# More products of constants around the gathered sums of an expert stage, and the first slot's products ahead of the second slot's turn

## The chip, the core and the metric

The kernel runs on one core of one Trainium2 chip. The metric is the device time of one execution in microseconds, the median of several runs. TensorE, VectorE (DVE in the profile), ScalarE (ACT), GpSimd (POOL) and the SP queue each work through a list of their own; they wait for each other by semaphores only. The granted clock of TensorE in the profile is a share of 2.4 GHz: 1.00 is 2.4 GHz, 0.50 is 1.2 GHz.

## What is computed

Two blocks of two transformer layers each, float32, batch 1, 256 tokens, model width 1024. The first block has two kinds of attention and a dense MLP per layer. The second has a pooling layer and an attention layer, each followed by a mixture of experts, and it is in these two mixtures that the change lies:

```python
def hier_moe(h, w_rg, b_rg, w_re, b_re, w_gate, w_up, w_down):
    ...
    gates = jnp.sum(jax.nn.one_hot(expert_id, N_EXPERTS, dtype=jnp.float32) * e_w[..., None], axis=1)
    a = jnp.einsum('nd,edf->nef', hf, w_gate)
    b = jnp.einsum('nd,edf->nef', hf, w_up)
    hid = jax.nn.silu(a) * b * gates.astype(h.dtype)[..., None]
    return jnp.einsum('nef,efd->nd', hid, w_down).reshape(shp)
```

Each token has two experts out of 16 (both in one of four groups), each expert 256 hidden columns. In layer 0 the mixture has 512 tokens (the latent set and the context set, four tiles of 128), in layer 1 it has 256 (two tiles).

## The kernel before

Every engine has a program of its own, and the order of its work is written out by hand; a claim of a PSUM bank waits for whoever read the bank last (`claim`, `freed`).

An expert stage (`moe`, L1045 for TensorE, L1621 for ScalarE, L2300 for VectorE, L2522 for GpSimd) works in slots of 128 rows: 23 slots in layer 0, 19 in layer 1. Slots 0 to 15 are one expert each; further slots take what is over and gather their weights too. First the tokens are routed and their rows written to memory. Then for each slot s:

- GpSimd gathers 128 token rows into `h_row[s % 3]` (L2534), three slots ahead; the gather for slot s + 3 waits until the turning of slot s has read its buffer.
- TensorE turns them, 8 transposes into PSUM banks 0 and 1 (`turn_rows`, L1089, instructions at L1094). It claims both banks, so it waits for VectorE's reading of the slot before.
- ScalarE copies the turned rows to the high part (`rows_high`, L1646) and VectorE subtracts to get the low part (`rows_low`, L2306).
- TensorE multiplies with the gate and up weights (`gates_and_ups`, L1098): for each of 8 pieces of the depth a product high by high, low by high and high by low, 24 in all. The low parts of the rows are waited for before the third product.
- ScalarE's tanh, two steps of VectorE and a turning of the hidden values follow, and the down products (`downs`) of slot s stand behind the gate and up products of slot s + 1.

Weights come through a ring of four buffers `raw`, filled by the SP queue; ScalarE rounds them (`round_expert`) and VectorE splits off the low part (`split_expert`, L1874). For the first slots ScalarE's and VectorE's order is written out ahead of the loop.

After the last slot GpSimd gathers, for each tile of 128 tokens, the two expert rows of each token (`both`, L2569). ScalarE scales the first by its gate, VectorE adds the second (L2353), TensorE turns the sum (8 transposes at L1166), and VectorE adds it into x (`add_tile`, 8 instructions at L2347). In layer 0 ScalarE then squares x and TensorE sums the squares over features (`sum_tile`, 8 one-column matmuls for each tile, 16 instructions in the profile), and `norm` spreads the reciprocal root. In layer 1 TensorE turns x back and ScalarE copies it out (`store`).

`idle(b, n)` (L665) issues n products of constants, 128 by 512, into bank b, which nobody reads. Each shows as two instructions. One such block of 8 stands after the last slot. All matmuls are issued from the helper at L663.

Of the kernel before, what the change touches and what calls it, by code (L numbers as in the profile page):

```python
# [322 lines left out]
def build(nc, a, out):  # L323
    with ExitStack() as ctx:
# [330 lines left out]
        def tensor_program(e):  # L655
            freed = {}

            def claim(b):
                for sig, name in freed.pop(b, ()):
                    e.wait_ge(*sig.at(*name))  # L660
# [4 lines left out]
            def idle(b, n):  # L665

                claim(b)
                for _ in range(n):
                    mm(psum[:, b, :], ident, cst[:, C_ROT1:C_ROT1 + 512], True, True)
# [329 lines left out]
            s = split_slot(g)  # L999
# [45 lines left out]
            def moe(layer):  # L1045
# [43 lines left out]
                def turn_rows(s):  # L1089
                    claim(0)  # L1090
                    claim(1)
                    e.wait_ge(*in_h_row[s % 3].at(layer, s))
                    for k in range(DT):
                        d = e.transpose(psum[:, k // 4, k % 4 * P:(k % 4 + 1) * P], h_row[:, s % 3, k:D:DT], ident)  # L1094
                    d.then_inc(*turned.on("row", layer, s))
                    freed[0] = freed[1] = [(rest, ("ht", layer, s))]
# [47 lines left out]
                    freed[5] = freed[6] = [(copied, ("y", layer, s))]  # L1144

                turn_rows(0)
                turn_rows(1)
                for s in range(slots + 1):
                    if s < slots:
                        gates_and_ups(s)  # L1150
                    if s:
                        turn_hidden(s - 1)
                    if s + 2 < slots:
                        turn_rows(s + 2)
                    if s:
                        downs(s - 1)

                idle(7, 8)

                for i in range(T):  # L1160
                    b = 2 * (i % 2)
                    claim(b)
                    claim(b + 1)
                    e.wait_ge(*shaped.at("both", layer, i))
                    for k in range(DT):
                        d = e.transpose(psum[:, b + k // 4, k % 4 * P:(k % 4 + 1) * P],  # L1166
                                        both[:, 2 * i, k * P:(k + 1) * P], ident)
                    d.then_inc(*turned.on("both", layer, i))
                    freed[b] = freed[b + 1] = [(added, ("both", layer, i))]
                    if layer == 0 and i:  # L1170
                        sum_tile(i - 1)
                    if layer == 1 and i:
                        store(i - 1)
                if layer == 0:
                    sum_tile(T - 1)
                    norm(("q", 0))
                    idle(4, 1)
                else:
                    store(T - 1)
# [154 lines left out]
        def scalar_program(e):  # L1334
# [286 lines left out]
            def moe(layer):  # L1621
                stage = ("e", layer)
                T, slots = 2 * len(NORMS[stage][0]), SLOTS[layer]
                for t in range(DT):
                    modulate(stage, t)
                e.wait_ge(*turned.at("logit_rows", layer))
                e.activation(logit_rows[0:20, 0:T * P], psum[0:20, 4, 0:T * P], ACT.Copy).then_inc(
                    *copied.on("logit_rows", layer))
                for i in range(T):
                    b = 2 * (i % 2)  # L1630
                    o = tmp[:, 2 * i:2 * i + 2, :]
                    e.wait_ge(*turned.at("h_row", layer, i))
                    e.activation(o, psum[:, b:b + 2, :], ACT.Copy).then_inc(*copied.on("h_row", layer, i))
                    e.wait_ge(*copied.at("h_row", layer, i))
                    e.dma_start(h_dram[layer][i * P:(i + 1) * P, :], o.rearrange("p b c -> p (b c)")).then_inc(
                        *h_kept.on(layer, i))
                e.wait_ge(*routed.at("shifted", layer))
                e.activation(ROUTE[layer]["eg"], ROUTE[layer]["d4"], ACT.Exp).then_inc(*expd.on("group", layer))
                e.wait_ge(*routed.at("dm", layer))
                e.activation(ROUTE[layer]["ex"], ROUTE[layer]["dm"], ACT.Exp).then_inc(*expd.on("pair", layer))  # L1640
                if layer == 1:
                    e.wait_ge(*multiplied.at(WO + 3))
                round_expert("g", layer, 1)
                round_expert("u", layer, 1)

                def rows_high(s):  # L1646
                    e.wait_ge(*turned.at("row", layer, s))
                    e.activation(ht_hi[:, s % 2], psum[:, 0:2, :].rearrange("p b (k c) -> p (b k) c", c=P),
                                 ACT.Copy).then_inc(*rounded.on("ht", layer, s))

                e.wait_ge(*routed.at("all", layer))
                rows_high(0)
                rows_high(1)
                for s in range(slots + 1):
                    if s < slots:
                        e.wait_ge(*multiplied.at("gu", layer, s))
                        e.activation(tmp[:, s % 2, 0:UC], psum[:, 2 + s % 2, 0:UC], ACT.Tanh, scale=0.5).then_inc(
                            *copied.on("tanh", layer, s))
                    if s:
                        at_ = (s - 1) % 2  # L1660
                        e.wait_ge(*turned.at("hid", layer, s - 1))
                        e.activation(ut_all[:, at_, :], psum[:, 4, 0:P], ACT.Copy).then_inc(  # L1662
                            *copied.on("ut", layer, s - 1))
                        e.activation(ut_hi[:, at_, :], psum[:, 4, P:2 * P], ACT.Copy).then_inc(
                            *rounded.on("ut", layer, s - 1))
                    if s + 2 < slots:
                        rows_high(s + 2)
                        round_expert("g", layer, s + 2)
                    if s < slots:
                        round_expert("d", layer, s)  # L1670
                    if s + 2 < slots:
                        round_expert("u", layer, s + 2)
                    if s:
                        at_ = (s - 1) % 2
                        e.wait_ge(*multiplied.at("d", layer, s - 1))
                        if s >= 3:
                            e.wait_ge(*y_kept[at_].at(layer, s - 3))
                        e.activation(y_row[at_][:], psum[:, 5:7, :].rearrange("p b c -> p (b c)"), ACT.Copy).then_inc(
                            *copied.on("y", layer, s - 1))
                        e.wait_ge(*copied.at("y", layer, s - 1))  # L1680
                        e.dma_start(y_dram[layer][(s - 1) * P:s * P, :], y_row[at_][:]).then_inc(
                            *y_kept[at_].on(layer, s - 1))
                if layer == 0:
                    feed(QKV - 1)

                def square_tile(i):
                    e.wait_ge(*added.at("both", 0, i))
                    e.activation(tmp[:, 2 * i:2 * i + 2, :].rearrange("p b (k c) -> p (b k) c", c=P),
                                 x[:, :, i * P:(i + 1) * P], ACT.Square).then_inc(*copied.on("sq_tile", i))

                def store(i):
                    e.wait_ge(*turned.at("out", i))
                    e.activation(tmp[:, 2 * i:2 * i + 2, :], psum[:, 4 + 2 * i:6 + 2 * i, :], ACT.Copy).then_inc(
                        *copied.on("out", i))

                for i in range(T):
                    e.wait_ge(*in_both[i].at(layer, 1))
                    e.activation(both[:, 2 * i, :], both[:, 2 * i, :], ACT.Copy,
                                 scale=gate_w[:, 0, i:i + 1]).then_inc(*copied.on("both", layer, i))
                    if layer == 0 and i:  # L1700
                        square_tile(i - 1)
                if layer == 0:
                    square_tile(T - 1)
                    norm_root(("q", 0))
                else:
                    for i in range(T):
                        store(i)
# [97 lines left out]
        def vector_program(e):  # L1805
# [494 lines left out]
            def moe(layer):  # L2300
# [9 lines left out]

                rows_low(0)
                split_expert("g", layer, 1)
                rows_low(1)
                split_expert("u", layer, 1)
                for s in range(slots + 1):
                    if s:
                        at_ = (s - 1) % 2
# [335 lines left out]
```

## Time and profile before

| | us |
|---|---|
| median of 3 runs | 1694.5 (1692.42 to 1698.91) |
| the profiled execution, device time | 1690.77 |
| its span in the profile | 1689.0 |
| granted clock, mean | 0.951 |
| TensorE busy | 1523.5 (90%) |
| VectorE busy | 1284.8 (76%) |
| ScalarE busy | 859.9 (51%) |
| GpSimd busy | 222.9 (13%) |

Times in the text are microseconds from the start of the span. A row of the timeline gives start, duration, engine, line, operation, output and inputs with their shape, how many instructions were merged into it, and in brackets how long the engine had been idle and what ended that. Durations of merged rows run from the first start to the last end.

### The profile page before, as it was taken

To read this page: it belongs to the slowest core of one execution; us is meant where nothing else is said; L and a number is where in the kernel's file an instruction comes from. 1 tells how busy PE (TensorE), PEld (TensorE's weight loads), DVE (VectorE), ACT (ScalarE), POOL (GpSimd) and SP (SyncE) were. 2 spreads that over 40 slices of the span, in tenths; PEclk is the share of its full clock that TensorE was granted. 3 is DMA by queue.
4 is the path that set the end of the run, shared out by engine and by line. 5 is a ranking of instruction groups with operands and counts; after the bars stand their busy time and mean duration, and the time that the engine had idled before them with its cause. 6 is when DMAs were issued, how large, how long until landed. Compare 5 with 4: busy or idle time off the path is not lost.

```text
span 1689.0 us, 24256 instructions
## 1 busy us (share of the span) xinstructions
PE 1523.5 (90%) x9830; PEld 1295.2 (77%) x9830; DVE 1284.8 (76%) x1882; ACT 859.9 (51%) x1186; POOL 222.9 (13%) x201
## 2 busy tenths in 40 slices
PE   3999989999999987999998889989979889799996
PEld 2889878999888977899887567767668547577764
DVE  4968878787877988899885668877658883588872
ACT  2546435444444642544444447766534464377762
POOL 5040010000004000000000311013220300311021
PEclk9999999999999998999999889999969899899998
DMA  9753687899763555578772369999965531599973
GB/s 324 267 170 128 222 299 265 299 325 313 269 200 126 176 174 194 191 268 279 263 259 75 125 224 415 422 413 358 363 219 200 179 121 50 209 393 423 423 307 137
DMA packets 191871, 424.99 MB, mean 252 GB/s; under 512 B 8344, under 2 KB 136784, under 8 KB 175504
## 3 DMA queue, kind: packets, MB, share of 16 engines
q1 hardware_dynamic: 170688, 334.53, 55.6%
q0 software_dynamic: 13824, 63.61, 10.1%
q10 hardware_dynamic: 7248, 25.30, 3.7%
q8 instruction: 78, 1.28, 0.3%
q14 instruction: 33, 0.27, 0.0%
HBM read 397.19 MB, written 26.21 MB: 251 GB/s over the span
## 4 chain that ended last, share of the span: by engine, by line
PE 57%; DVE 24%; DMA 7%; ACT 7%; issue 3%; POOL 1%; SPq 0%; POOLq 0%; ACTq 0%; DVEq 0%
PE psum L663 54%; DVE acc L1871 6%; DVE w_lo L1850 6%; DMA h_row<-h_rows,token_at 3%; PE psum L1094 2%; DVE gu_lo L1883 2%; ACT w_hi L1361 2%; DMA raw<-in_w_ada 1%; ACT att_room L1783 1%; DVE tmp L2054 1%; DVE tmp L1904 1%; ACT gu_hi L1375 1%; DVE stats L2060 1%; DMA dn_raw<-in_moe_wd 1%; DVE h_lo L1913 1%
## 5 line engine op out<-in xcount | busy, mean ns | idle before, releaser
L1850 DVE TENSOR_TENSOR w_lo<-raw,w_hi 128x1024 fp32r<-128x1024 f32 x250 | 302.2, 1251 | 66.3 <-ACT w_hi L1361 66.2
L663 PE MATMUL psum<-h_lo,w_hi 128*128 128x256 f32 (+1 forms) x1280 | 339.5, 289 | 2.8 <-DVE h_lo L2099 2.8
L663 PE MATMUL psum<-h_hi,w_lo 128*128 128x256 f32 (+1 forms) x1280 | 339.3, 288 | 0.2 <-DVE w_lo L1850 0.2
L1871 DVE SCALAR_TENSOR_TENSOR acc<-raw,cond,acc 128x1024 f32<-128x1024 f32 x224 | 294.5, 1324 | 11.5 <-DMA raw<-in_w_ada 6.5
L1361 ACT ACTIVATE w_hi<-raw 128x2048 fp32r<-128x2048 f32 x125 | 238.8, 1912 | 121.3 <-PE psum L663 90.1
L663 PE MATMUL psum<-h_hi,w_hi 128*128 128x256 f32 (+1 forms) x1280 | 262.9, 298 | 18.0 <-DVE tmp L2082 14.5
L663 PEld LDWEIGHTS psum<-h_lo,w_hi 128*128 128x128 f32 x1280 | 248.8, 194 | 4.3 <-DVE h_lo L2099 3.0
L663 PEld LDWEIGHTS psum<-h_hi,w_lo 128*128 128x128 f32 x1280 | 248.9, 194 | 2.0 <-DVE w_lo L1850 0.6
L663 PEld LDWEIGHTS psum<-h_hi,w_hi 128*128 128x128 f32 x1280 | 199.2, 196 | 39.1 <-issue 16.3
L1883 DVE TENSOR_TENSOR gu_lo<-raw,gu_hi 128x1024 fp32r<-128x1024 f32 x160 | 188.7, 1221 | 27.7 <-ACT gu_hi L1375 27.7
L1375 ACT ACTIVATE gu_hi<-raw 128x2048 fp32r<-128x2048 f32 x84 | 159.7, 1905 | 0.8 <-PE psum L663 0.8
L663 PE MATMUL psum<-gu_lo,ht_hi 128*128 128x512 f32 x336 | 132.4, 394 | 0.0
L663 PE MATMUL psum<-gu_hi,ht_lo 128*128 128x512 f32 x336 | 132.2, 393 | 0.0
L663 PE MATMUL psum<-u_lo,w_hi 128*128 128x256 f32 x448 | 121.7, 288 | 9.3 <-DVE u_lo L2127 9.3
L663 PE MATMUL psum<-gu_hi,ht_hi 128*128 128x512 f32 x336 | 126.2, 396 | 0.0
L663 PE MATMUL psum<-u_hi,w_lo 128*128 128x256 f32 x448 | 121.1, 287 | 0.0
L2438 POOL TENSOR_TENSOR tmp<-tmp 128x256 f32<-128x256 f32 (+1 forms) x28 | 29.9, 1069 | 543.0 <-ACT tmp L1386 542.9
L663 PE MATMUL psum<-u_hi,w_hi 128*128 128x256 f32 x448 | 100.4, 290 | 0.0
L663 PEld LDWEIGHTS psum<-u_lo,w_hi 128*128 128x128 f32 x448 | 87.8, 196 | 10.3 <-DVE u_lo L2127 10.3
L663 PE MATMUL psum<-dn_raw,ut_all 128*128 128x512 f32 x168 | 83.1, 618 | 5.6 <-ACT ut_all L1662 5.3
L663 PEld LDWEIGHTS psum<-u_hi,w_lo 128*128 128x128 f32 x448 | 87.7, 196 | 0.0
L1386 ACT ACTIVATE tmp<-x 128x256 f32<-128x256 f32 (+1 forms) x56 | 25.8, 476 | 104.0 <-DVE x L1984 90.7
(259 smaller groups left out, 2771.2 us busy)
## 6 DMA issues: line engine op xcount, KB each, us to landing
raw<-in_w_ada SPq DMA_DIRECT2D x48, 1024.0 KB, 6.6
raw<-in_w_mod SPq DMA_DIRECT2D x48, 1024.0 KB, 5.6
raw<-in_w_in SPq DMA_DIRECT2D x34, 1024.0 KB, 5.7
raw<-in_w_up SPq DMA_DIRECT2D x32, 1024.0 KB, 5.5
raw<-in_w_down SPq DMA_DIRECT2D x32, 1024.0 KB, 6.8
raw<-in_moe_wg SPq DMA_DIRECT2D x32, 1024.0 KB, 11.5
raw<-in_moe_wu SPq DMA_DIRECT2D x32, 1024.0 KB, 10.4
dn_raw<-in_moe_wd SPq DMA_DIRECT2D x32, 1024.0 KB, 10.1
```

What stands on the lines that cost most here:

```text
L663: return e.matmul(o, lhs, rhs, start=start, stop=stop, skip_group_check=True)
L1094: d = e.transpose(psum[:, k // 4, k % 4 * P:(k % 4 + 1) * P], h_row[:, s % 3, k:D:DT], ident)
L1361: e.activation(flat_unit(w_hi[:, split_slot(u)]), raw[:, slot, :], ACT.Copy).then_inc(*w_rounded.on(u))
L1375: e.activation(gate_up(0, s, kind == "u"), raw[:, p % RAW_SLOTS, :].rearrange("p (k c) -> p k c", c=UC), ACT.Copy).then_inc(*w_rounded.on( ...
L1386: e.activation(tbuf(i, n), x[:, t, 0:n], ACT.Square).then_inc(*copied.on("sq", stage, t))
L1783: e.activation(att_room[:, h % 4, qt * S2:(qt + 1) * S2], psum[:, 2 * (h % 2) + qt, :], ACT.Exp, bias=st[:, 2 + qt:3 + qt], scale=scale[:, ...
L1850: e.tensor_tensor(flat_unit(w_lo[:, split_slot(u), k]), raw[:, slot, part], plain(flat_unit(w_hi[:, split_slot(u), k])), ALU.subtract).the ...
L1871: e.scalar_tensor_tensor(out=a_buf, in0=src[:, k, :], scalar=s, in1=a_buf, op0=ALU.mult, op1=ALU.add).then_inc(*mod_v.on(p, n, k))
L1883: e.tensor_tensor(gate_up(1, s, kind == "u")[:, k], src[:, k], plain(gate_up(0, s, kind == "u")[:, k]), ALU.subtract).then_inc(*w_rest.on( ...
L1904: e.scalar_tensor_tensor(out=tmp[:, t % 4, c], in0=x[:, t, c], scalar=gain_col(row, chunk + 1, t), in1=psum[:, 5, c], op0=ALU.mult, op1=AL ...
L1913: e.scalar_tensor_tensor(out=lo[:, t - 1, c], in0=tmp[:, (t - 1) % 4, c], scalar=column(row, chunk, t - 1), in1=plain(hi[:, t - 1, c]), op ...
L2438: e.tensor_tensor(o, o, tbuf(4 + (t + 1) % 4, n), ALU.add).then_inc(*pooled.on("sq", stage, t))
```

## The change

TensorE: slot 1's turning is issued behind slot 0's gate and up products. The block of constant products after the last slot grows from 8 to 15. One more constant product follows each turning of a gathered tile, in both layers; in layer 0 two more stand ahead of the last tile's sums and one ahead of the norm. ScalarE: the copy of slot 1's turned rows stands behind the tanh of slot 0. VectorE: the split of slot 1's up weights stands ahead of the subtraction for slot 1's rows. The results are the same.

```diff
@@ TensorE @@
                 turn_rows(0)
-                turn_rows(1)
                 for s in range(slots + 1):
                     if s < slots:
                         gates_and_ups(s)
+                    if s == 0:
+                        turn_rows(1)
                     if s:
                         turn_hidden(s - 1)
                     if s + 2 < slots:
...
-                idle(7, 8)
+                idle(7, 15)
...
                     d.then_inc(*turned.on("both", layer, i))
+                    idle(7, 1)
                     freed[b] = freed[b + 1] = [(added, ("both", layer, i))]
...
                 if layer == 0:
+                    idle(7, 2)
                     sum_tile(T - 1)
+                    idle(7, 1)
                     norm(("q", 0))
                     idle(4, 1)
@@ ScalarE @@
                 rows_high(0)
-                rows_high(1)
                 for s in range(slots + 1):
                     if s < slots:
                         e.wait_ge(*multiplied.at("gu", layer, s))
                         e.activation(tmp[:, s % 2, 0:UC], psum[:, 2 + s % 2, 0:UC], ACT.Tanh, scale=0.5).then_inc(
                             *copied.on("tanh", layer, s))
+                    if s == 0:
+                        rows_high(1)
@@ VectorE @@
                 rows_low(0)
                 split_expert("g", layer, 1)
+                split_expert("u", layer, 1)
                 rows_low(1)
-                split_expert("u", layer, 1)
```

## Rows read from the trace of the kernel before

**Rows 1.** The page, its chain that ended last: shares of the span by engine.
```profile
PE 57%; DVE 24%; DMA 7%; ACT 7%; issue 3%; POOL 1%; SPq 0%; POOLq 0%; ACTq 0%; DVEq 0%
```

**Rows 2.** The timeline (start, duration, what) at the start of layer 0's slots.
```profile
985.64 1.12 PE L1094 MATMUL psum<-cst,h_row 128*128 128x128 f32 x8
986.86 1.02 ACT L1648 ACTIVATE ht_hi<-psum 128x1024 fp32r<-128x1024 f32 x1 [12.52 <-PE psum L1094]
...
987.91 1.22 DVE L2308 TENSOR_TENSOR ht_lo<-psum,ht_hi 128x1024 fp32r<-128x1024 f32 x1 [5.41 <-ACT ht_hi L1648]
...
989.19 1.16 PE L1094 MATMUL psum<-cst,h_row 128*128 128x128 f32 x8 [2.43 <-DVE ht_lo L2308]
...
990.63 1.59 POOL L2535 DMA_INDIRECT h_row<-h_rows,token_at  x1 [2.18 <-PE psum L1094]
990.78 0.63 PE L663 MATMUL psum<-gu_hi,ht_lo 128*128 128x512 f32 x1
...
997.30 1.05 PE L1094 MATMUL psum<-cst,h_row 128*128 128x128 f32 x8
...
998.11 0.71 PE L663 MATMUL psum<-gu_hi,ht_hi 128*128 128x512 f32 x2
```

**Rows 3.** The timeline at the start of layer 1's slots.
```profile
1463.08 1.12 PE L1094 MATMUL psum<-cst,h_row 128*128 128x128 f32 x8 [1.59 <-DMA h_row<-h_rows,token_at]
...
1466.63 1.97 PE L1094 MATMUL psum<-cst,h_row 128*128 128x128 f32 x8 [2.43 <-DVE ht_lo L2308]
...
1469.26 0.63 PE L663 MATMUL psum<-gu_hi,ht_lo 128*128 128x512 f32 x1
```

**Rows 4.** Windows: stretch, length, busy PE, PEld, DVE, ACT, POOL (instructions), clock, DMA share, GB/s.
```profile
963.10:966.50 3.40, 3.40 (x26) 2.67 (x25) 2.88 (x16) 2.25 (x3) 0.00 (x0) 1.00 0.37 151
987.00:990.30 3.30, 1.11 (x9) 1.11 (x10) 2.39 (x3) 0.88 (x1) 0.94 (x1) 1.00 0.63 215
990.50:993.70 3.20, 3.20 (x9) 2.50 (x8) 3.15 (x3) 0.92 (x1) 1.59 (x1) 0.50 0.43 110
1465.00:1471.50 6.50, 4.87 (x16) 4.20 (x17) 5.29 (x5) 1.34 (x2) 1.87 (x2) 0.50 0.61 187
```

**Rows 5.** The timeline at the end of layer 0's experts.
```profile
1227.11 7.03 PE L663 MATMUL psum<-cst 128*128 128x512 f32 x16
...
1241.17 1.97 PE L1166 MATMUL psum<-cst,both 128*128 128x128 f32 x8 [7.03 <-DVE both L2353]
...
1243.93 2.15 DVE L2347 SCALAR_TENSOR_TENSOR x<-psum,mod,x 128x128 f32<-128x128 f32 x8
...
1252.75 3.57 PE L663 MATMUL psum<-cst,tmp 128*128 128x1 f32 x16
...
1254.97 2.15 DVE L2347 SCALAR_TENSOR_TENSOR x<-psum,mod,x 128x128 f32<-128x128 f32 x8
...
1258.17 2.16 DVE L2347 SCALAR_TENSOR_TENSOR x<-psum,mod,x 128x128 f32<-128x128 f32 x8 [1.05 <-PE psum L1166]
...
1265.82 2.08 PE L663 MATMUL psum<-cst,rstd_col 128*128 128x128 f32 x8 [0.56 <-DVE rstd_col L1890]
```

**Rows 6.** Windows, the same columns, the end of layer 0's experts.
```profile
1241.00:1266.00 25.00, 21.84 (x97) 20.18 (x98) 12.52 (x37) 9.00 (x9) 1.88 (x2) 0.50 0.70 251
```

**Rows 7.** The timeline at the end of layer 1's experts.
```profile
1663.45 7.03 PE L663 MATMUL psum<-cst 128*128 128x512 f32 x16
...
1676.41 1.97 PE L1166 MATMUL psum<-cst,both 128*128 128x128 f32 x8 [5.92 <-DVE both L2353]
...
1679.25 4.30 DVE L2347 SCALAR_TENSOR_TENSOR x<-psum,mod,x 128x128 f32<-128x128 f32 x16
```

**Rows 8.** Layer 0's later slots: TensorE's waits for gathered rows (sum, times, longest); gathers' landing.
```profile
PE psum L1094 <- DMA h_row<-h_rows,token_at: 6.2, 4, 4.8
DMA to landing us min/median/max: 6.9/8.4/12.6
```

**Rows 9.** Windows, the same columns, one slot in the middle of layer 1.
```profile
1532.20:1541.90 9.70, 9.70 (x45) 7.53 (x44) 8.12 (x10) 7.33 (x9) 0.94 (x1) 1.00 1.01 420
```

## The prediction

> **What bounds the kernel now.** I read the page first [rows 1]: TensorE carries 57% of the chain that ended last, so what counts is when TensorE's queue gets to go on. The change touches only the two expert stages, and each of them in two places: the start, where the rows of the first two slots are turned, and the end, where the experts' outputs are gathered and added. I read both places in the timeline and then the granted clock in the windows.
>
> At the start of layer 0 the turning of slot 0 runs at 985.64, and the turning of slot 1 only at 989.19, because both write PSUM banks 0 and 1: in between ScalarE copies (986.86, 1.02 us) and VectorE subtracts (987.91, 1.22 us), and TensorE waits 2.43 us [rows 2]. From one turning to the next it is 3.55 us. Layer 1 shows the same 3.55 us, 1463.08 to 1466.63 [rows 3]. Slot 0's own products stand behind slot 1's turning. The gap is followed by a stretch at a granted clock of 0.50, that is 1.2 GHz in place of 2.4: some 3.4 us in layer 0, and from 1465 to about 1471.7 in layer 1 [rows 4].
>
> At the end of layer 0 TensorE has nothing to do from 1234.14 (end of 8 products of constants, 7.03 us) until the first gathered and added tile is there at 1241.17 [rows 5]. From then to about 1270 it runs at 0.50 [rows 6]. But it isn't the bound of that loop: VectorE's first three additions into x start 5.52 us apart, the first at 1243.93, the third at 1254.97, in a ring VectorE, ScalarE's square, ScalarE's scaling, VectorE. Only the last addition (1258.17) waited for TensorE, 1.05 us, and behind it the sums and the norm are TensorE's own [rows 5]. Layer 1's end is short: the first turning starts at 1676.41, the two additions run from 1679.25 to 1683.55 [rows 7].
>
> **The start: slot 0's products ahead of slot 1's turning.** Gain: slot 0's products can start once ScalarE has copied row block 0. Two high products go, then the third, which reads the low part, waits for VectorE, whose subtraction ends at 989.13. So the third product starts where the second turning starts now, 989.2 in place of 990.78: 1.6 us earlier in layer 0 [rows 2]. In layer 1 it is 1466.6 in place of 1469.26, 2.6 us, but that time lies in the stretch at 0.50, which does half the work, so it is worth 1.3 us [rows 3, 4]. Loss: the turnings of slots 1 and 2 are now neighbours behind the products, and both write banks 0 and 1, so the 3.55 us from turning to turning stands there, where today no wait is (slot 2 is turned at 997.30 and the next products start at 998.11) [rows 2]. The wait has been moved, not removed, and the new one is whole, while the old one is only partly gone. Sum: 3.55 - 1.6 = +1.95 us in layer 0, 3.55 - 1.3 = +2.25 us in layer 1, together **+4.2 us**.
>
> Where the other queues are moved past: ScalarE's copy of slot 1 stands behind the tanh of slot 0 (0.38 us, started 0.2 us after the products end), which runs beside the turning (1.05 us): nothing. VectorE splits the second expert's up weights before slot 1's subtraction: these no longer wait 1.2 us, and their ring buffer is free for the SP queue that much earlier; no one waits for it. VectorE now sits waiting behind the split until slot 0's products are through, and queued behind that wait are the two steps of slot 0's hidden values (0.42 us each); they run while TensorE turns slot 2 and ScalarE copies it (2.1 us), and their reader comes a whole product block later: nothing. GpSimd's gather of row block 4 waits for slot 1's turning (now 990.63) and is issued some 8 us later, and its own queue with it; its reader is the turning of slot 4, behind two further blocks of products, at 9.70 us a slot some 16 us after the issue [rows 2, 9], and the longest landing of such a gather is 12.6 us [rows 8]: nothing. If the landing were longer the difference would be paid.
>
> The clock at the start. The trace has no wait between dense products of this length with both sides at 2.4 GHz, so I bound it. Today's stretches at 0.50 hold 3.2 us of TensorE's work in layer 0 and 4.9 us in layer 1, so they cost about 1.6 and 2.5 us [rows 4]. After the change the old gap is smaller (1.1 us, two products, 0.7 us) and may leave the clock up; the new gap of 2.43 us may drop it in slot 1's products. Both old dips gone and no new one: -4.1 us; both old ones kept and two new ones of 1.6 us: +3.2 us. A 2.43 us wait dropped the clock both times it is seen, so I expect the dips to move with the wait and take 0.
>
> Could the transfers hide the loss? In the loop TensorE is busy for all of the 9.70 us per slot and the DMA share is 1.01 beside it [rows 9]; later in layer 0 TensorE waits 6.2 us in all for gathered rows, and one gather took 12.6 us to land [rows 8]. A TensorE that comes 2 us later finds the queues that much less behind, if they never ran dry. But the share is only 0.43 to 0.63 around the start of both layers [rows 4], and the transfers are issued by the steps that come late. So between 0 and all of the 4.2 us hidden; I take 0.
>
> **The end: 7 more products before the first turning.** One costs 7.03 / 8 = 0.88 us, 0.86 from issue to issue. Seven take 6.0 us and end at 1240.1 in layer 0 (the wait ends at 1241.17) and, from 1663.45, at 1676.3 in layer 1 (1676.41): they fit, the second by 0.1 us [rows 5, 7]. If they end late, the first turning has room: it ends at 1678.4 and the addition starts at 1679.25, behind VectorE's own sum of the next tile. For the same reason a first turning in 1.1 in place of 1.97 us gains nothing in either layer. The cover of the seven is the gather; without it they would cost 6 us per layer.
>
> **The products between the tiles.** Layer 0 gets 1 after each turning, 2 before the last sum and 1 before the norm; layer 1 gets 1 after each turning. Clock held at 2.4 GHz through layer 0's end: a turning is 1.05 us, a product 0.86, a tile's sums half of 3.57, so TensorE needs 3.7 us of each 5.52. The sums of tile 2 start behind its square, about 1258.3, and end at 1260.1; two products, 1261.8; the last square is done by then (its addition starts at 1257.2); sums, 1263.6; a product, 1264.4; the norm starts there in place of 1265.82 and is 1.0 us shorter: **-2.5 us** [rows 5]. Clock left at 0.50: a turning 1.97, a product twice 0.86, the sums 3.57 [rows 5], together 7.2 us for a ring of 5.52, so TensorE becomes the bound: sums of tile 0 end at 1251.3, of tile 1 at 1258.5, of tile 2 at 1265.7, two products to 1269.1, sums to 1272.6, a product to 1274.3, norm there and not at 1265.82: **+8.5 us**. Which? Turnings and one-column sums alone have not raised it: 25 us at 0.50 with TensorE 87% busy [rows 6]. But four tiles turned with one product of constants in their middle stayed at 1.00 (963.1 to 966.5, the token rows being turned in the routing) [rows 4]. One product in every 5.5 us is between these two rows, so I expect the clock to fall at some tile and come back before the norm. I take +1 us, nearer to the held end.
>
> The Trainium skill, "TensorE: Matmul & The Clock Gate", Part 4 (PE-mode transpose), says that the full clock does not engage for transposes. The stretch from 1241 agrees (0.50 for 25 us); the row at 963.1 speaks against its strict form. By that rule the turnings would do nothing to hold the clock, and the end would come out at +8.5 in place of +1: rival B below.
>
> Layer 1's end: the output hangs on VectorE's second addition, which ends at 1683.55 [rows 7], and a store turning behind it. The product behind the second turning ends before the first addition does if the clock is held: 0. At 0.50 its 1.7 us delay both store turnings, the second of them too: up to +1.7 us. I take 0.
>
> **Sum**: +4.2 (start) + 0 (clock there) + 1 + 0 = +5.2 us on the profiled execution's own 1690.8 us, 1696.0 us. The median of the three runs lies 3.7 us above that execution; on it the forecast is 1694.5 + 5 = **1699.5 us**, slower by 0.3%, which a measurement of this kernel can barely tell (about 0.5%, 8.5 us, is its limit).
>
> **Rivals.** (A) The clock gains pay for the moved wait: held through layer 0's end (-2.5) and the old dips gone without new ones (-4.1), with +4.2: -2.4 us, 1692. For it: the gap is broken up and the 14 products of layer 0 fill waits. Against: the new wait is as long as the old. Chance 0.24. It ends on the other side of mine: faster than before, from the point where the end is held and more than 1.7 us of today's 4.1 us of dips is saved. (B) The products run at 0.50 and become the bound at the end of layer 0: 4.2 + 8.5 + up to 1.7, some +13 us, 1707.5; for it the 25 us at 0.50, against it the row at 963.1. Chance 0.17. (C) Transfers absorb the moved wait: +1 us, 1695.5, for it the share of 1.01 in the loop, against it the shares at the start. Chance 0.12. (D) The change does nothing that shows, as the seven products are hidden and the clock falls anyway: that is inside (C)'s time. My forecast (+2 to +8.5) has 0.47.
>
> **Range.** From A to near B: 1691 to 1707. Chances: faster by over 0.5% would need A and more, 0.04; slower by over 0.5% (above 1703) is B and the top of the forecast, 0.20; the rest 0.76.
>
> **What would show it.** In the profile after: in both layers turning 0, two products, a short stall, the rest of slot 0's products; then turning 1 and turning 2 with 3.55 us from start to start and a TensorE wait of about 2.4 us for VectorE's subtraction between them. Slot 1's products of layer 0 start 2 us later against turning 0 than today's 12.47 us (985.64 to 998.11) [rows 2]. The first turning of the gathered tiles takes 1.1 us in place of 1.97; additions into x still 5.52 us apart. What would prove me wrong: no TensorE wait between turnings 1 and 2; additions over 6 us apart (then B); the wait for a gather gone or 2 us shorter (then C).

## The result, and the profile after

| | us |
|---|---|
| before, median | 1692.6 |
| changed kernel, median | 1699.9 |
| ratio | 1.0042, interval 1.0026 to 1.0059 (+7.1 us, +4.4 to +10.0) |
| the changed kernel's profiled execution, device time | 1693.25 |
| its span | 1691.4 |

The change makes the kernel slower by 0.4%, forecast was 0.3%. The profiled execution is one of the quick ones of its kernel, 6.7 us under the median, so the totals of the two profiles (1689.0 and 1691.4) differ by less than the kernels do. The two stretches that the change touches are read by themselves.

The start of layer 0's slots in the timeline of the changed kernel (start, duration, engine, operation; in brackets the idle time and its end), to be laid beside [rows 2]:

```profile
980.13 1.06 PE L1094 MATMUL psum<-cst,h_row 128*128 128x128 f32 x8
...
982.34 1.23 DVE L2313 TENSOR_TENSOR ht_lo<-psum,ht_hi 128x1024 fp32r<-128x1024 f32 x1 [5.13 <-ACT ht_hi L1652]
982.41 0.70 PE L663 MATMUL psum<-gu_hi,ht_hi 128*128 128x512 f32 x2 [1.22 <-issue]
...
983.62 0.50 PE L663 MATMUL psum<-gu_hi,ht_lo 128*128 128x512 f32 x1 [0.51 <-DVE ht_lo L2313]
...
988.74 1.05 PE L1094 MATMUL psum<-cst,h_row 128*128 128x128 f32 x8
...
992.16 1.35 PE L1094 MATMUL psum<-cst,h_row 128*128 128x128 f32 x8 [2.37 <-DVE ht_lo L2313]
...
993.17 1.20 PE L663 MATMUL psum<-gu_hi,ht_hi 128*128 128x512 f32 x2
```

Slot 0's products start right behind ScalarE's copy, two of them, a stall of 0.51 us, and the rest. But behind them stand turnings 1 and 2, 3.42 us apart (988.74 and 992.16), with TensorE waiting 2.37 us for VectorE in between. That wait stood between turnings 0 and 1 before, 2.43 us. From turning 0 to slot 1's first product it is 13.04 us (980.13 to 993.17); it was 12.47. Layer 1 is the same picture, with the old wait's place at 1464.57 to 1468.13 and the new wait at 1477.94:

```profile
1464.57 1.13 PE L1094 MATMUL psum<-cst,h_row 128*128 128x128 f32 x8 [1.73 <-DMA h_row<-h_rows,token_at]
...
1468.13 0.79 PE L663 MATMUL psum<-gu_hi,ht_lo 128*128 128x512 f32 x1 [0.45 <-DVE ht_lo L2313]
...
1474.52 1.05 PE L1094 MATMUL psum<-cst,h_row 128*128 128x128 f32 x8
...
1477.94 1.97 PE L1094 MATMUL psum<-cst,h_row 128*128 128x128 f32 x8 [2.38 <-DVE ht_lo L2313]
```

Windows of the changed kernel (stretch, length, busy time of PE, PEld, DVE, ACT, POOL with instructions, granted clock, DMA share, GB/s), to be laid beside [rows 4] and [rows 6]. The first two are slot 0's and slot 1's products in layer 0, the third and fourth the same in layer 1, the rest the end of layer 0's experts:

```profile
983.60:988.60 5.00, 4.98 (x22) 4.14 (x23) 4.50 (x4) 0.00 (x0) 0.00 (x0) 1.00 0.61 171
993.20:996.20 3.00, 3.00 (x9) 2.43 (x8) 1.23 (x1) 2.65 (x2) 0.94 (x1) 0.50 1.00 414
1467.30:1470.50 3.20, 2.75 (x8) 1.88 (x7) 3.20 (x4) 0.00 (x0) 0.20 (x1) 0.52 0.50 178
1478.20:1481.00 2.80, 2.80 (x12) 2.51 (x12) 0.43 (x2) 1.05 (x2) 0.81 (x1) 0.50 0.94 332
1237.30:1245.00 7.70, 5.28 (x33) 3.65 (x33) 3.79 (x10) 3.24 (x3) 1.78 (x2) 1.00 0.74 263
1246.40:1249.60 3.20, 3.20 (x15) 2.21 (x13) 1.51 (x6) 1.65 (x2) 0.00 (x0) 0.60 1.08 385
1253.50:1266.00 12.50, 12.26 (x39) 8.85 (x39) 2.18 (x9) 3.62 (x4) 0.00 (x0) 0.50 0.30 102
```

In layer 0 slot 0's products now run at 1.00 throughout and slot 1's begin at 0.50: the slow stretch has gone along with the wait. In layer 1 the old slow stretch, from 1465 to about 1471.7 before, is shorter, and a new one has come.

The end of layer 0's experts, beside [rows 5]:

```profile
1237.34 1.09 PE L1167 MATMUL psum<-cst,both 128*128 128x128 f32 x8 [1.02 <-DVE both L2358]
...
1240.25 2.15 DVE L2352 SCALAR_TENSOR_TENSOR x<-psum,mod,x 128x128 f32<-128x128 f32 x8
...
1251.28 4.22 DVE L2352 SCALAR_TENSOR_TENSOR x<-psum,mod,x 128x128 f32<-128x128 f32 x16
...
1254.57 3.57 PE L663 MATMUL psum<-cst,tmp 128*128 128x1 f32 x16 [0.24 <-ACT tmp L1693]
...
1258.01 3.76 PE L663 MATMUL psum<-cst 128*128 128x512 f32 x4
1261.56 3.41 PE L663 MATMUL psum<-cst,tmp 128*128 128x1 f32 x16
1264.84 2.05 PE L663 MATMUL psum<-cst 128*128 128x512 f32 x2
...
1266.68 1.91 PE L663 MATMUL psum<-cst,rstd_col 128*128 128x128 f32 x8
```

The 15 products end 1.02 us ahead of the first gathered tile, and its turning takes 1.09 in place of 1.97 us. The additions still come 5.5 us apart (1240.25 to 1251.28 is two rings of 5.52), and the last one now follows at once, where it waited 1.05 us. Then the gain is lost again: by the last sums the clock has fallen to 0.50 once more, and the two products (3.76 us) and the one ahead of the norm (2.05 us) stand on the path. From the first gathered turning to the norm it is 29.34 us (1237.34 to 1266.68), before 24.65 (1241.17 to 1265.82).

In layer 1 the block fits to the tenth that was worked out: the first turning follows it with no idle time, and nothing moves behind it (12.6 us to the end in both).

### The profile page after: what moved, and what is told of

Same layout as the page of the kernel before. It is cut to its first block, busy times and chain, and to the rows that moved or that the text cites. A ratio compares the mean times of both kernels' runs of the same rounds, so it can differ in the third digit from the quotient of the medians.

```text
span 1691.4 us, 24346 instructions
## 1 busy us (share of the span) xinstructions
PE 1531.6 (91%) x9876; PEld 1291.8 (76%) x9876; DVE 1284.1 (76%) x1882; ACT 860.4 (51%) x1186; POOL 222.9 (13%) x201
## 3 DMA queue, kind: packets, MB, share of 16 engines
q0 software_dynamic: 13824, 63.61, 10.1%
## 4 chain that ended last, share of the span: by engine, by line
PE 56%; DVE 25%; DMA 7%; ACT 7%; issue 3%; POOL 1%; SPq 0%; POOLq 0%; ACTq 0%; DVEq 0%
PE psum L663 53%; DVE acc L1876 6%; DVE w_lo L1855 6%; DMA h_row<-h_rows,token_at 3%; PE psum L1094 2%; ACT w_hi L1365 2%; DMA raw<-in_w_ada 1%; DVE gu_lo L1888 1%; DMA raw<-in_w_down 1%; ACT att_room L1788 1%; DVE steps_room L1948 1%; DVE tmp L2059 1%; DVE tmp L1909 1%; DVE stats L2065 1%; DMA dn_raw<-in_moe_wd 1%
## 5 line engine op out<-in xcount | busy, mean ns | idle before, releaser
L2313 DVE TENSOR_TENSOR ht_lo<-psum,ht_hi 128x1024 fp32r<-128x1024 f32 x42 | 51.4, 1224 | 43.2 <-ACT ht_hi L1652 43.1
## 6 DMA issues: line engine op xcount, KB each, us to landing
raw<-in_moe_wu SPq DMA_DIRECT2D x32, 1024.0 KB, 10.1
```

The costliest lines, as they stand in the source:

```text
L2313: e.tensor_tensor(ht_lo[:, s % 2], psum[:, 0:2, :].rearrange("p b (k c) -> p (b k) c", c=P), plain(ht_hi[:, s % 2]), ALU.subtract).then_in ...
```

## The experiments

The totals move by at most 0.42%, and their intervals reach 0.15% to 0.27% to either side, so each run is read twice: by its ratio, and by the stretches of its profile. Each row is one profile, and a stretch differs from one execution to the next too. All in one place, in us, from the profiles' timelines; T is a turning of gathered rows, so T0 to T3 is the start, T0 to last the whole loop of slots, and "end" runs from the first turning of a gathered tile to the norm in layer 0:

```
kernel               T0-T3     T0-T3     T0-last   T0-last   end       ratio (interval)
                     layer 0   layer 1   layer 0   layer 1   layer 0
before               18.26     19.01     213.10    172.05    24.65
changed              20.32     21.48     213.91    172.86    29.34     1.0042 (1.0026 to 1.0059)
e1_order             20.25     22.63     217.38    174.96    24.84     1.0032 (1.0017 to 1.0047)
e2_consts            16.55     18.65     213.36    171.00    27.38     1.0024 (0.9998 to 1.0050)
e3_block15           16.56     18.25     211.25    170.79    24.72     1.0007 (0.9989 to 1.0025)
e4_tiles             18.24     18.27     214.39    171.67    23.68     0.9999 (0.9980 to 1.0017)
e5_banks             15.53     16.68     209.62    168.78    25.04     0.9971 (0.9944 to 0.9997)
e6_banks_order       17.35     17.43     210.90    169.75    25.40     0.9998 (0.9972 to 1.0024)
e7_order_fill        18.71     21.13     215.24    173.28    25.14     1.0017 (0.9995 to 1.0039)
e8_two_per_tile      16.59     18.92     212.81    171.94    21.79     1.0001 (0.9979 to 1.0022)
e9_banks_two         15.52     18.07     213.05    171.71    21.94     0.9965 (0.9942 to 0.9988)
e10_one_per_tile     16.58     17.90     212.16    170.92    23.39     1.0003 (0.9986 to 1.0021)
e11_on_path          16.58     18.22     212.10    170.66    29.69     1.0009 (0.9986 to 1.0032)
```

### The two halves of the change

The order alone:

```diff
 turn_rows(0)
-turn_rows(1)
 for s in range(slots + 1):
     if s < slots:
         gates_and_ups(s)
+    if s == 0:
+        turn_rows(1)
...
```

(with ScalarE's and VectorE's order moved as in the change.)

> Only the moved turning of slot 1 (with ScalarE's and VectorE's order), the products of constants as before. My theory (the wait between two turnings is moved, not removed): turning 0 to turning 3 takes 2 to 2.5 us longer in each layer, and all of it reaches the end: +4.2 us. Rival C (later transfers absorb it): turning 0 to turning 3 is 2 to 2.5 us longer just so, but turning 0 to the last slot's turning only about 0.8 us, as in the profile of the changed kernel, and the kernel is only +1.6 us. In both cases the end of layer 0 is that of before: first gathered turning to norm about 24.7 us.

Measured: +0.32%, 5.4 us (2.9 to 8.0). The wait is there as in the changed kernel, in its timeline at the three turnings:

```profile
986.54 1.05 PE L1094 MATMUL psum<-cst,h_row 128*128 128x128 f32 x8
995.15 1.05 PE L1094 MATMUL psum<-cst,h_row 128*128 128x128 f32 x8
998.58 1.97 PE L1094 MATMUL psum<-cst,h_row 128*128 128x128 f32 x8 [2.37 <-DVE ht_lo L2310]
```

By its median the moved wait is the larger part of the loss. In layer 0 T0 to T3 is 2.0 us longer than in the one profile of before. Against the mean of the seven profiles with the old order and the old banks (17.05 and 18.46 us), the mean of the new order's two (20.29 and 22.06) is 3.2 and 3.6 us longer. The old order shows 16.6 us in five of its seven profiles of layer 0 and 18.25 in two: in layer 0 the old slow stretch isn't always there. In layer 1 it is there in all seven.

Over the whole loop of slots (means 212.74 and 171.29 against 215.65 and 173.91) 2.9 and 2.6 us of the 3.2 and 3.6 arrive. A part of what is missing can be placed: from turning 3 to turning 4 it is 10.1 us in all seven profiles of the old order and 9.7 us in both of the new, in both layers, so 0.4 us per layer comes back at once. With a spread of 3 us in layer 0's loop alone the profiles don't settle whether more is absorbed. The total is the stronger evidence: its interval starts at 2.9 us, above the 1.6 us that rival C gave for this run. The +0.8 us per layer that the changed kernel's own profile shows against that of before lies within the spread.

The products of constants alone:

```diff
-idle(7, 8)
+idle(7, 15)
...
     d.then_inc(*turned.on("both", layer, i))
+    idle(7, 1)
...
 if layer == 0:
+    idle(7, 2)
     sum_tile(T - 1)
+    idle(7, 1)
     norm(("q", 0))
```

> Only the products of constants (8 to 15, one per tile, 2 and 1 ahead of the last sums and the norm), the order as before. Prediction's term: +1 us, between -2.5 (clock held) and +8.5 (clock at 0.50 through layer 0's end). Rival after the changed kernel's profile: the clock falls in the middle, first gathered turning to norm in layer 0 takes 27 to 30 us in place of 24.65, so +3 to +5 us. The starts of the layers are those of before (turning 0 to turning 1 3.55 us).

Measured: +0.24%, 4.1 us (-0.3 to 8.5), and the end of layer 0 2.7 us longer. The stretch is the rival's figure (27 to 30 us), not that of the prediction's +1 us; the total doesn't tell the two apart. Together the two halves give +0.56%, and the whole +0.42%, which their intervals allow.

### Which products cost

Only the block:

```diff
-idle(7, 8)
+idle(7, 15)
```

> Only the block after the last slot grows from 8 to 15 products. My step: hidden behind the gather, first turning of the gathered tiles 1.1 in place of 1.97 us, nothing gained behind it: 0 us, last slot's turning to first gathered turning as before (42.4 and 41.3 us). Rival: the products themselves run late or at half clock and hold up the first turning: up to +2 us per layer.

Only the other ones:

```diff
     d.then_inc(*turned.on("both", layer, i))
+    idle(7, 1)
...
 if layer == 0:
+    idle(7, 2)
     sum_tile(T - 1)
+    idle(7, 1)
     norm(("q", 0))
```

> The block stays at 8, only the products between the gathered tiles, ahead of the last sums and ahead of the norm. If these products at 0.50 are what costs (rival B), the clock has fallen before the first turning, as in the kernel before, and the end of layer 0 is longest here: first gathered turning to norm 29 to 33 us, kernel +5 to +8.5 us. If they bring the clock back early (rival A), 22 to 25 us and 0 to -2 us.

Measured: the block +0.07% and an end of 24.72 us, so it is hidden and gives nothing, as worked out. The mark that I had named for it is off in layer 0: from the last slot's turning to the first gathered one it is 44.68 us, not 42.4. The block isn't the cause, since TensorE had finished it 1.02 us before and waited for the gathered tile, and the run `e7_order_fill` with the old block shows 45.06:

```profile
1244.73 1.09 PE L1166 MATMUL psum<-cst,both 128*128 128x128 f32 x8 [1.02 <-DVE both L2353]
```

The other products -0.01% and 23.68 us. The clock was at 0.50 ahead of the first tile, as expected, but came back at the second turning (1241.8 to 1251.8 at 1.00). It fell once more at the last tile and was up again for the products on the path:

```profile
1256.78 1.96 PE L663 MATMUL psum<-cst 128*128 128x512 f32 x4
1258.58 1.84 PE L663 MATMUL psum<-cst,tmp 128*128 128x1 f32 x16
1260.28 1.10 PE L663 MATMUL psum<-cst 128*128 128x512 f32 x2
```

I had taken the long end as the likelier one, and it was wrong for this execution. Whether the shorter block brings this about or the execution did isn't shown: it is one profile.

The same with the three on the path apart:

```diff
-idle(7, 8)
+idle(7, 15)
...
     d.then_inc(*turned.on("both", layer, i))
+    idle(7, 1)
```

> The changed kernel's products of constants without the two ahead of the last sums and the one ahead of the norm; order as before. If these three are what makes the end of layer 0 longer, first gathered turning to norm falls from 27.4 and 29.3 us (with them) to 22 to 25 us, and the kernel is 0 to -2 us against before. If the clock's fall between the tiles is what costs, it stays at 26 us or more.

```diff
 if layer == 0:
+    idle(7, 2)
     sum_tile(T - 1)
+    idle(7, 1)
     norm(("q", 0))
```

> Only the two products ahead of the last sums and the one ahead of the norm, everything else as before. The clock is at 0.50 there, so two products take 3.4 us and one 1.7 us of which 0.6 lies in the wait for the root: +4.6 us by the norm (29.2 in place of 24.65), less if the products bring the clock back before the last sums (half of 3.5 us) and the norm (1 us): then 26.5. Kernel +2 to +4.6 us. If they were hidden behind ScalarE's square: 24.7 and 0.

Measured: without the three the end is 23.39 us; with only the three it is 29.69, +5.0 us. The timeline of the latter, from the last sums but one to the norm:

```profile
1259.00 3.58 PE L663 MATMUL psum<-cst,tmp 128*128 128x1 f32 x16
1262.44 3.76 PE L663 MATMUL psum<-cst 128*128 128x512 f32 x4
1265.99 3.41 PE L663 MATMUL psum<-cst,tmp 128*128 128x1 f32 x16
1269.27 2.05 PE L663 MATMUL psum<-cst 128*128 128x512 f32 x2
1271.11 1.91 PE L663 MATMUL psum<-cst,rstd_col 128*128 128x128 f32 x8
```

At 0.50 the two products cost 3.55 us from issue to issue (1262.44 to 1265.99), and the sums behind them take 3.41 us, no quicker than those ahead of them (3.58). The clock didn't come back in time to pay for them. The changed kernel's end has the same four figures to 0.01 us. So the loss at the end sits in these three products, where they run at 0.50: with them the end is 27.38, 29.34 and 29.69 us in three profiles (in `e2_consts`, the 27.38, the last of them was already at 1.00), and 23.68 in `e4_tiles`, where all three ran at 1.00. The ones behind the turnings are harmless and shorten the end by about 1.3 us in the one profile that has them alone. What they do to the clock shows beside `e3_block15`, which differs only in them: there the clock fell 2.8 us after the first gathered turning began (0.50 from 1247.6 on), here it stayed at 1.00 for 9.3 us (1241.50 to 1250.80).

The totals of the two runs (+0.03%, +0.09%) can't tell 1 us, nor 5 us with certainty (1.0032 is 5.4 us). The profiles say that what happens in the end is not given back up to layer 1's slots: from the first gathered turning of layer 0 to turning 0 of layer 1 it is 227.2 us in the changed kernel, 227.1 with the three alone and 225.4 in `e2_consts`, against 220.9 to 223.6 in the six profiles without products between the tiles.

Two products per tile, none on the path:

```diff
-idle(7, 8)
+idle(7, 15)
...
     d.then_inc(*turned.on("both", layer, i))
+    idle(7, 2)
```

> 15 products in the block, then 2 behind each gathered turning and none ahead of the last sums or the norm; order as before. If the loss of the constants lies in the products on the path ahead of the last sums and the norm, and the clock can be held by more of them where TensorE waits anyway, the first gathered turning to the norm of layer 0 falls to 21.5 to 23 us (24.7 before): -2 to -3 us. If two per tile run at 0.50 they make TensorE the bound: a tile takes up to 9 us, the norm comes at 35 us, +10 us.

Measured: the end is 21.79 us, 2.9 us shorter, the gain that was expected if the clock is held; it was at 1.00 but for 1251.4 to 1254.9:

```profile
1255.57 1.84 PE L663 MATMUL psum<-cst,tmp 128*128 128x1 f32 x16
1257.27 1.07 PE L1166 MATMUL psum<-cst,both 128*128 128x128 f32 x8
1258.18 1.88 PE L663 MATMUL psum<-cst 128*128 128x512 f32 x4
1259.90 3.96 PE L663 MATMUL psum<-cst,tmp 128*128 128x1 f32 x32
```

Both of the last sums together take 3.96 us; before it was 6.99. The ratio (1.0001, 0.9979 to 1.0022, so -3.6 to +3.7 us) doesn't show it and doesn't exclude it. Up to layer 1's turning 0 it is kept: 218.7 us from the first gathered turning, 221.9 before.

### What the moved wait is made of

Slot 1 turned into other banks, the order of before:

```diff
 def turn_rows(s):
-    claim(0)
-    claim(1)
+    b = 5 if s == 1 else 0
+    claim(b)
+    claim(b + 1)
...
-    freed[0] = freed[1] = [(rest, ("ht", layer, s))]
+    freed[b] = freed[b + 1] = [(rest, ("ht", layer, s))]
```

(ScalarE and VectorE read the same banks.)

> Order and products of constants of the kernel before, but slot 1 is turned into PSUM banks 5 and 6, which nobody uses yet. My theory (the start is held by the two banks that both turnings write): turning 1 follows turning 0 by about 1 us in place of 3.55, slot 0's third product waits for VectorE's subtraction alone, and turning 0 to turning 3 is 1.5 us shorter in each layer with the clock as it was, up to 3 us if the dip behind the wait goes: -3 to -6 us in all. Rival (the gathered rows of slot 1 or the transfers hold the start): turning 1 comes no earlier than 3 us and nothing is gained.

The same with the order of the change:

> The moved turning of the changed kernel, with the products of constants of before, and slot 1 turned into banks 5 and 6. If the whole cost of the move is the wait for banks 0 and 1 behind it, the 2.4 us of TensorE's wait between turnings 1 and 2 goes, about 0.9 us of it comes back as a wait of slot 1's third product for VectorE, and turning 0 to turning 3 falls from 20.3 and 22 us to 17.4 to 18.5 us: the kernel -3 to 0 us against the one before, 5 to 8 us below the run with the order alone. If the loss has another cause, it stays near +5.

Measured: with the old order T0 to T3 falls to 15.53 and 16.68 us and the kernel is 0.29% faster (0.03% to 0.56%, 4.9 us). With the new order it falls from 20.25 and 22.63 to 17.35 and 17.43 us, and the loss is gone (0.9998). Part of that fall is the clock, which is at 1.00 through both starts of this run. In the timeline of the run with the new order:

```profile
986.68 1.05 PE L1095 MATMUL psum<-cst,h_row 128*128 128x128 f32 x8
...
995.28 1.95 PE L1095 MATMUL psum<-cst,h_row 128*128 128x128 f32 x16
997.45 0.73 PE L663 MATMUL psum<-gu_hi,ht_hi 128*128 128x512 f32 x2 [0.21 <-ACT ht_hi L1651]
998.71 0.50 PE L663 MATMUL psum<-gu_hi,ht_lo 128*128 128x512 f32 x1 [0.52 <-DVE ht_lo L2313]
```

Turnings 1 and 2 run as one row of 16, and slot 1's products wait 0.21 and 0.52 us, 0.7 in place of 2.37. So the wait is that for the two banks, shown from both sides. What I had wrong: in the run with the old order turning 1 comes 2.47 us behind turning 0, not 1 us, and with no slow stretch in layer 0 the start is 1.0 us shorter than the old order's 16.56, not 1.5:

```profile
984.74 1.05 PE L1095 MATMUL psum<-cst,h_row 128*128 128x128 f32 x8
...
987.21 1.12 PE L1095 MATMUL psum<-cst,h_row 128*128 128x128 f32 x8 [1.42 <-DMA h_row<-h_rows,token_at]
988.08 0.72 PE L663 MATMUL psum<-gu_hi,ht_hi 128*128 128x512 f32 x2
```

With the banks free, the gathered rows of slot 1 are the next late thing, 1.1 us ahead of the banks.

The wait filled, in the order of the change:

```diff
     if s == 0:
         turn_rows(1)
+        idle(7, 2)
```

> The order alone, and two products of constants in the 2.4 us wait between turnings 1 and 2 (they need 1.7 us). It parts the wait from the clock: the wait stays, TensorE isn't idle in it. If the stretch at 0.50 in slot 1's products comes from the wait, it goes, and turning 0 to turning 3 falls by 1.6 us to about 18.7 (layer 0); kernel +2 to +3 us against before. If the clock falls in any case, 20.3 us and +5 as with the order alone.

Measured, in layer 0:

```profile
1003.69 1.05 PE L1094 MATMUL psum<-cst,h_row 128*128 128x128 f32 x8
1004.58 1.88 PE L663 MATMUL psum<-cst 128*128 128x512 f32 x4
1007.12 1.16 PE L1094 MATMUL psum<-cst,h_row 128*128 128x128 f32 x8 [0.65 <-DVE ht_lo L2311]
```

and its clock behind that (window, columns as above):

```profile
1007.50:1013.80 6.30, 6.30 (x33) 5.36 (x33) 4.19 (x5) 5.49 (x5) 0.94 (x1) 1.00 0.89 363
```

From turning to turning it is 3.43 us as without them, the wait is filled, and slot 1's products run at 1.00. T0 to T3 is 18.71 us, 1.5 less than with the order alone: the slow stretch came from the wait, and costs about as much as one half of the 3.0 us seen at 0.50. What is left is the moved wait by itself: against the 16.56 us of the old order, with no slow stretch on either side, +2.15 us, where the prediction had worked out +1.95. In layer 1, where the clock falls ahead of slot 0's products too, 21.13 against 22.63. The total (+0.17%, -0.05% to +0.39%) lies where expected, without telling it from the order alone.

### A version that beats both

Banks 5 and 6 for slot 1, the order of before, and two products behind each turning (the edits of `e5_banks` and `e8_two_per_tile` together):

> The two parts that point to a gain together: slot 1 turned into banks 5 and 6 (order of before), 15 products in the block, 2 behind each gathered turning, none ahead of the last sums and the norm. If the local gains add up (about 2 to 3 us in each start, 2 to 3 us from the first gathered turning to the norm), -0.3% to -0.5%: 5 to 8 us below before. If the end's gain is given back later, as the unchanged total of the run with two per tile may say, it stays at the -0.3% of the banks alone.

Measured: 0.35% faster than before (0.12% to 0.58%, 5.9 us), with an end of 21.94 us and a start of 15.52 and 18.07 us. It is faster than both kernels; how much the products add to the banks' 0.29% is below what the totals tell.

## Why the prediction was right, point by point

**The moved wait, +4.2 us.** Right in place, in cause and nearly in size. The new wait of 2.37 us stands between turnings 1 and 2, the third product starts 3.49 us behind turning 0 (980.13 to 983.62), as worked out, and the order alone costs 5.4 us. The mark that I named for it, slot 1's first product 2 us later against turning 0, shows only 0.57 us (13.04 against 12.47) in this pair of profiles, since slot 0's products ran at 0.50 in the one of before and at 1.00 in that of after; the mark left the clock out. The banks as its cause are shown by `e5_banks` and `e6_banks_order`.

**The clock at the start, taken as 0.** Too low. The trace of before had the slow stretch in both layers, so I let the old ones pay for the new ones. Layer 0's old one is missing in five of seven profiles (layer 1's in none), while the new one was there in all four starts with an unfilled new wait. Against the means, T0 to T3 is +6.8 us in both layers together and T0 to T4 +6.0; less the 4.2 us of the wait, the term should have been +2 to +3 us. The mistake in the reading was to take a stretch that depends on how the execution falls as a fixed cost of the kernel, from one profile.

**Transfers absorb, taken as 0.** 5.5 of the 6.8 us arrive at the last slot; 0.8 us come back between turnings 3 and 4, and the rest is within the spread. Rival C as a whole is excluded: by it the order alone would cost 1 to 1.6 us, and it costs 5.4, at least 2.9. That a smaller part is absorbed isn't excluded. GpSimd's gather of row block 4 is issued 9.93 us after turning 0 (990.06) in place of 4.99, 4.9 us later and not the 8 that I had counted, and turning 4 doesn't wait for it, as I had said.

**The seven products, 0.** Right in both layers, to 0.1 us, and nothing is gained behind them.

**The products between the tiles, +1 us.** Right that they fall between the held clock and 0.50, and that TensorE doesn't become the bound (rings stay at 5.5 us; rival B fell). Mis-sized: 2.7 us in `e2_consts` and 4.7 in the changed kernel, both from profiles, since no total resolves this term. I had counted them as one lot. The single ones cost nothing and bring about 1.3 us; the three on the path cost 5.0 us where the clock is at 0.50, and in the changed kernel it was there when it mattered: it came back at about 1269.5, behind the norm's start at 1266.68 and not before it. In `e4_tiles` it did come back in time, so +1 us or less is possible too, in one profile of four.

**Layer 1's end, 0.** Right: about 12.6 us from the first gathered turning to the end of the span in both (1676.41 to 1689.0, 1678.77 to 1691.4).

**The sum.** +5.2 us forecast, 7.1 measured (4.4 to 10.0): the interval takes in the forecast, though the two clock terms were both too low. Read from the profiles, the start (6.0) and the end (2.7 to 4.7) add up to 8.7 to 10.7 us, more than the totals show, so the sum is no proof of its terms. What the totals show clearly is the order's loss; that the products of constants add to it rests on the stretches, as the whole is only 0.10% above the order alone and the intervals overlap. And that 1699.5 us was forecast and 1699.9 measured is luck: the base, a median of three runs, was 1.9 us above that of twenty (1694.5 and 1692.6), and the change was about 2 us larger than forecast. Rival A, the clock paying for the wait, is seen in pieces (slot 0's products at 1.00, the last addition without its wait) and falls as a whole.

The Trainium skill, "TensorE: Matmul & The Clock Gate", Part 4 (PE-mode transpose), says that the full clock does not engage for transposes. Where only turnings and one-column sums follow the block, the trace agrees: `e3_block15` is at 0.50 from 1247.60 to 1269.40. The end at 0.50 throughout and the +8.5 us that I had drawn from it didn't come: the changed kernel's row 1237.30:1245.00, two turnings, two constant products and the sums of tile 0, is at 1.00. What turnings count for by themselves isn't shown.

## What to carry to other kernels

A step that is moved takes its wait along if what it waits for is a buffer that its neighbour uses: look at who is its neighbour in the new place, and change the buffer rather than the order. Filler products belong where the engine waits anyway, and are to be sized for the slow clock too; three of them on the path cost more than the clock they brought in three of four profiles. And where parts of a kernel differ by microseconds from one execution to the next, compare stretches between two marks, over several profiles, ahead of totals.

## What the runs showed of the hardware

The first turning of layer 0 starts between 980.1 and 995.1 us in thirteen profiles, though nothing is changed ahead of it in any of them. These 15 us are twice the whole effect of the change; their cause wasn't tried. And a TensorE wait of only 2.4 us, with a turning of about 1 us on each side, was followed by about 3 us at a granted clock of 0.50 in all four starts of the new order, 0.8 us behind its end in layer 0 of the changed kernel (wait to 992.16, 1.00 up to 992.9, 0.50 from 993.2 to 996.2). From slot 0's last product to slot 1's first it is 4.3 us there (988.9 to 993.17). With 1.9 us of constant products in the wait there was no such stretch, in either layer. It isn't certain to come: the old wait, as long and with turnings on both sides too, stood in layer 0 without one in five of seven profiles.
